# Delta-rule mixer: two chains over four groups in units of two tiles per direction, or four chains of 128 channels in units of one tile per direction

## The chip, the cores and the metric

The program runs on one core of a Trainium2 chip. The time is device microseconds from start to end of one execution. A core has TensorE (PE, with its weight loads listed as PEld), VectorE (DVE), ScalarE (ACT), GpSimd (POOL) and SyncE (SP, which issues the DMAs here). Each engine runs its own instructions in order, and the engines wait for one another through semaphores.

## The reference

Two transformer-like blocks are computed. The change lies in one mixer of the first block, a delta rule with decay (RWKV-7) over 8 heads of 64 channels, 256 context and 1024 latent tokens, run forwards (d = 0) and backwards (d = 1). The outputs of both directions are added and normed per head:

```python
def _rwkv7_scan(r, w, k, v, a, b, s0, reverse, emit):
    def step(s, inp):
        r_t, w_t, k_t, v_t, a_t, b_t = inp
        sa = jnp.einsum('bhvk,bhk->bhv', s, a_t)
        s = s * w_t[:, :, None, :] + sa[..., None] * b_t[:, :, None, :] + v_t[..., None] * k_t[:, :, None, :]
        y = jnp.einsum('bhvk,bhk->bhv', s, r_t) if emit else None
        return s, y
...
    y = ys[0] + ys[1]
    mu = jnp.mean(y, axis=-1, keepdims=True)
    var = jnp.mean(jnp.square(y - mu), axis=-1, keepdims=True)
    yn = ((y - mu) * lax.rsqrt(var + RW_GN_EPS)).reshape(bsz, l, RW_WIDTH) * lnx_g + lnx_b
    yn = yn + (bonus[0] + bonus[1]).reshape(bsz, l, RW_WIDTH)
    g = jax.nn.sigmoid(gd) @ g2
    return (yn * g).astype(r.dtype), (states[0], states[1])
```

## The kernel before

The program is a row of stages with a barrier between them (modulation, first projection, `rwkv_mix`, `hgrn_mix`, routing, experts, second block). Only `rwkv_mix` (tiles named rwmix_...) is touched. It is written out in full, without loops on the engines.

**Work.** Tokens are cut in chunks of 64. Within a chunk the recurrence is a triangular system. Its inverse is built in five levels by doubling: at each level `w` multiplies T by the masked X (tile W, plus the unit matrix), and `t` multiplies TT by W and W by TT to give the next T and its transpose TT. Then come w and u (tile wu), the matrices m and n by which a chunk changes the state, the state steps c0, c1, ..., and the outputs. Channels are cut in four groups of 128 (two heads each).

**Units.** A unit is a pair of tiles of each direction (4 chunks for each direction, 2 heads) of one group. Two chains, u = 0 and 1, each with its own half of PSUM, work off two groups one after the other, 5 units for each group, 20 units in all. Operations on DVE, ACT and POOL are mostly 128 partitions by 512 columns.

**Order.** A unit is a list of slots (`turn`, `prodb`, `prodk`, `zed`, `t0`, `w1`, `t1`, ..., `t5`, `wup`, `mn`, `intra`, `c0`, `query`, `c1`, `c2`, `c3`, `inter`). All engines walk the same interleaving (`interleaved`): one slot of chain 0, then one of chain 1, which is OFFSET = 11 slots behind. Below, one such step over all chains is called a round. A PE slot writes PSUM, and DVE or ACT copies the result to SBUF before the chain's next slot can run.

**Products.** Most matmuls are 64 by 64 with 64 columns. `crossed` (L1162) spreads them over the four quadrants of the array; `intra` (L1252, L1253), `zed` (L1211) and `wup` (L1172) use the two quadrants on the diagonal. The copies of T are on ACT (L1298), those of TT on DVE (L1370). The sums of outputs go through ACT (yi, L1313), POOL (L1469, second half of a group) and DVE (yacc, L1409).

**Norm.** When a group is done, the chain's last unit ends with the norm over all its 1024 tokens in slots `mean` to `gate`, in operations of 1024 columns (L1416 to L1432 on DVE, L1319 to L1328 on ACT, L1286 on PE, L1474 and L1476 on POOL); then SP stores the group.

**Loads.** SP loads a unit two ahead, tensor by tensor, 12 DMAs for each (L1129 to L1132), among them the decays of whole chunks (tot) in the layout in which DVE uses them.

## Time and profile before

| | us |
|---|---|
| median of three runs | 3963.1 (3958.7 to 3964.5) |
| span of the profiled execution | 3941.6 |
| so around the span | 21.5 |
| first DMA issue of `rwkv_mix` | 771.7 |
| first DMA issue of the next stage | 1358.7 |
| `rwkv_mix`, from one to the other | 587.0 |

The rows are from one profiled execution, and each time in them is counted from the start of its span. In a row of the timeline the first number is the start, the second the time until the last instruction of the row ends, `x` the number of instructions, and the bracket the idle time of that engine ahead of it with what ended it ("issue" is a wait for nothing that the profile shows). One float32 matmul of the code is two PE instructions in the trace, each with its own weight load; a transpose is one.

### The profile page before, as it was taken

How to read it: one execution, taken by the hardware profiler on the slowest of the kernel's cores; microseconds unless marked ns; L12 is line 12 of the kernel's file. 1: busy time of each engine (PE TensorE's matmuls, PEld its weight loads, DVE VectorE, ACT ScalarE, POOL GpSimd, SP SyncE). 2: the span in 40 equal slices, each digit the busy share in tenths (PEclk: the TensorE clock that was granted, in tenths of full speed). 3: DMA queues.
4: the chain of work that ended last, by engine and by line, in shares of the span. 5: the costliest groups of instructions: out<-in, count | busy, mean ns of one | idle time of the engine just before them, and what ended most of it. 6: DMA issues, size and time to landing. Idle time of an engine off the chain costs nothing. (4 is left out here: it accounts for less than half of the span.)

```text
span 3941.6 us, 97846 instructions
## 1 busy us (share of the span) xinstructions
PE 3377.2 (86%) x38463; PEld 2331.6 (59%) x38463; DVE 2360.6 (60%) x4245; ACT 1768.8 (45%) x2361; POOL 731.1 (19%) x706
## 2 busy tenths in 40 slices
PE   4999799677778587979998998999689999878789
PEld 0899788577677475733332333333267777666567
DVE  1688688655555466627776766776377574056631
ACT  0577577422222124307776766776222321156620
POOL 4000000043444200331221221222112333200000
PEclk7999899899899788989999999999899999988899
DMA  8354445421221255949889999953734323265452
GB/s 315 84 171 139 160 130 166 159 86 46 61 72 44 82 167 200 209 155 315 277 263 356 351 354 357 326 160 76 244 87 128 86 75 96 95 153 132 117 181 75
DMA packets 520291, 665.36 MB, mean 169 GB/s; under 512 B 77168, under 2 KB 423984, under 8 KB 516768
## 3 DMA queue, kind: packets, MB, share of 16 engines
q1 hardware_dynamic: 494576, 572.44, 45.2%
q0 software_dynamic: 25216, 86.62, 8.9%
q8 instruction: 312, 5.11, 0.5%
q14 instruction: 139, 1.14, 0.1%
q10 hardware_dynamic: 48, 0.05, 0.0%
HBM read 493.08 MB, written 165.94 MB: 167 GB/s over the span
## 5 line engine op out<-in xcount | busy, mean ns | idle before, releaser
L2600 PE MATMUL routed_p_gu<-routed_fixed,routed_x 128*32 128x512 f32 x3840 | 572.5, 600 | 0.0
L2600 PE MATMUL routed_p_gu<-moe_exp_w,routed_x 128*32 x1280 | 571.5, 600 | 0.7 <-DVE routed_fixed L2722 0.7
L2654 ACT COPY routed_fixed<-moe_exp_w 128x1024 f32 x320 | 332.6, 1047 | 222.1 <-DMA moe_exp_w<-in_exp_w_up_dram 86.3
L2722 DVE COPY routed_fixed<-moe_exp_w 128x1024 f32 x640 | 398.0, 681 | 51.3 <-DMA moe_exp_w<-in_exp_w_up_dram 42.9
L544 PE MATMUL front_ps<-front_a_high,front_w_high 128*128 128x320 f32 (+1 forms) x1120 | 362.7, 324 | 16.3 <-DVE front_w_low L797 13.4
L544 PE MATMUL front_ps<-front_a_low,front_w_high 128*128 128x320 f32 (+1 forms) x1120 | 353.8, 316 | 0.0
L544 PE MATMUL front_ps<-front_a_high,front_w_low 128*128 128x320 f32 (+1 forms) x1120 | 353.7, 316 | 0.0
L2600 PEld LDWEIGHTS routed_p_gu<-moe_exp_w,routed_x 128*32 128x32 f32 x1280 | 135.4, 111 | 356.2 <-issue 356.2
L3606 PE MATMUL pre_ps<-pre_a_high,pre_w_high 128*128 128x512 f32 x720 | 287.1, 399 | 13.3 <-ACT pre_xb L3753 6.7
L2615 PE MATMUL routed_p_y<-routed_wd,routed_hT 128*32 x640 | 290.4, 597 | 3.4 <-ACT routed_fixed L2665 3.4
L2615 PE MATMUL routed_p_y<-routed_fixed,routed_hT 128*32 128x512 f32 x1920 | 291.4, 597 | 0.0
L2734 DVE COPY routed_fixed<-routed_wd 128x1024 f32 x320 | 201.7, 691 | 141.2 <-PE routed_p_gu L2600 126.8
L3606 PE MATMUL pre_ps<-pre_a_high,pre_w_low 128*128 128x512 f32 x720 | 281.3, 391 | 0.0
L3606 PE MATMUL pre_ps<-pre_a_low,pre_w_high 128*128 128x512 f32 x720 | 281.2, 391 | 0.0
L2557 POOL DMA_INDIRECT total<-rw_mask,routed_yidx x80 | 128.6, 1608 | 732.2 <-ACT rw_mask L2671 604.6
L544 PEld LDWEIGHTS front_ps<-front_a_high,front_w_high 128*128 128x128 f32 x1120 | 213.3, 190 | 35.2 <-DVE front_w_low L797 18.0
L1445 POOL TENSOR_TENSOR rwmix_TT<-rwmix_at,rw_mask 64x256 f32<-64x256 f32 (+1 forms) x60 | 43.5, 725 | 922.4 <-DVE rwmix_at L1346 916.5
L544 PEld LDWEIGHTS front_ps<-front_a_low,front_w_high 128*128 128x128 f32 x1120 | 213.2, 190 | 1.3
L544 PEld LDWEIGHTS front_ps<-front_a_high,front_w_low 128*128 128x128 f32 x1120 | 213.0, 190 | 0.0
L2665 ACT COPY routed_fixed<-routed_wd 128x1024 f32 x160 | 167.1, 1047 | 47.4 <-PE routed_p_gu L2600 46.7
L2615 PEld LDWEIGHTS routed_p_y<-routed_wd,routed_hT 128*32 128x32 f32 x640 | 70.8, 111 | 196.9 <-issue 196.9
L3606 PEld LDWEIGHTS pre_ps<-pre_a_high,pre_w_high 128*128 128x128 f32 x720 | 135.9, 189 | 46.7 <-issue 16.5
(550 smaller groups left out, 7386.6 us busy)
## 6 DMA issues: line engine op xcount, KB each, us to landing
moe_exp_w<-in_exp_w_gate_dram SPq DMA_DIRECT2D x64, 1024.0 KB, 13.3
moe_exp_w<-in_exp_w_up_dram SPq DMA_DIRECT2D x64, 1024.0 KB, 16.4
routed_wd<-in_exp_w_down_dram SPq DMA_DIRECT2D x64, 1024.0 KB, 15.1
front_wt<-in_w_in_dram SPq DMA_DIRECT2D x70, 512.0 KB, 4.4
mod_w<-in_w_mod_dram SPq DMA_DIRECT2D x24, 1024.0 KB, 18.2
pre_wt<-in_w_in_dram SPq DMA_DIRECT2D x44, 512.0 KB, 4.0
out_a<-mix SPq DMA_DIRECT2D x24, 512.0 KB, 4.0
total<-out_none SPq DMA_DIRECT2D x24, 512.0 KB
```

The source lines that it names most:

```text
L544: op = nc.tensor.matmul(ps[:, s % 2, c, 0:size], w_part[:, s % 2, k, :], a_part[:, k, first + c * size:first + (c + 1) * size], start=(k = ...
L1445: nc.gpsimd.tensor_tensor(combos(TT[u][:])[to, es], combos(at[u][:])[at_rows, es], mask(MASK_LEVEL, at_rows, es), ALU.mult)
L2557: nc.gpsimd.indirect_dma_start(total, bass.IndirectOffsetOnAxis(ap=yidx[b % 2][:, :], axis=0), y[:, b % 2, :], None, compute_op=ALU.add).t ...
L2600: op = nc.tensor.matmul(p_gu[spot(s), :], x[:, b % 2, k, spot(s)], w, start=(k == 0), stop=(k == KD - 1))
L2615: op = nc.tensor.matmul(p_y[spot(s), h, :], hT[:, m, spot(s)], w, start=(m == 0), stop=(m == MT - 1))
L2654: nc.scalar.copy(fixed[:, place_of(b, c), 0, :], wgu[:, bass.ds(e % WS, 1), c * D:(c + 1) * D].rearrange("p o n -> p (o n)"))\
L2665: nc.scalar.copy(fixed[:, at, 0, :], wd[:, bass.ds(e % WD, 1), m, :].rearrange("p o n -> p (o n)"))\
L2722: op = nc.vector.tensor_copy(fixed[:, place_of(b, c), s - 1, :], wgu[:, bass.ds(es[s] % WS, 1), c * D:(c + 1) * D].rearrange("p o n -> p ( ...
L2734: op = nc.vector.tensor_copy(fixed[:, at, s - 1, :], wd[:, bass.ds(e % WD, 1), m, :].rearrange("p o n -> p (o n)"))
L3606: op = nc.tensor.matmul(ps[:, u, a:a + n], w_part[:, u, k, :], a_part[:, k, a:a + n], start=(k == 0 and j == 0), stop=(k == KD - 1 and j = ...
```

## The change

- **Chains.** Four chains, one for each group of 128 channels, each with two banks of PSUM, 5 slots apart (`OFFSET = 5`).
- **Units.** A unit is one tile of each direction (2 chunks for each direction): 10 units for each chain, then an eleventh that holds only a norm. Operations are 128 by 256 where they were 128 by 512, and there are twice as many.
- **State.** Two state steps for each unit (`c0`, `c1`), with both directions side by side on the two halves of the partitions.
- **Outputs.** The three products of an output (cb with u, ck with v, q with the state) add up in PSUM in slot `c1`; the copy through yi and its POOL addition are gone. They now all run on the two diagonal quadrants, as does the query product, and in `mn` the m products lie on the diagonal ones and the n products, twice as many, on the other two.
- **T and TT.** Both are written to one tile (`both`) by one ACT copy of 512 columns; the DVE copies of TT are gone.
- **Norm.** The norm of a unit's tiles is spread over the slots of the next unit, in operations of 256 columns (units 7 to 10, which then have 26 slots, the last one 8).
- **Loads.** a, b, r, k of one direction are one DMA. r is loaded once more in the layout of the state (`turned`). The decays are loaded once at the start by 16 DMAs and put in place by 40 POOL copies ahead of POOL's first mask, and the loads of lnx, for which ACT waits, come behind them.

```diff
-    OFFSET = 11
+    OFFSET = 5
...
         def slots(n):
-            out = ["turn", "prodb", "prodk", "zed", "t0"]
+            norm = ["mean", "square", "var", "root", "norm", "back", "res", "gate"] if finishing(n) else []
+            if n == TILES:
+                return norm
+            out = ["turn", "prod", "zed", "t0"] + norm[0:1]
             for l in range(1, LEVELS + 1):
-                out += [f"w{l}", f"t{l}"]
-            out += ["wup", "mn"] + (["intra"] if latent(n) else []) + ["c0"] + (["query"] if latent(n) else []) + ["c1", "c2"]
...
+                out += [f"w{l}"] + norm[2 * l - 1:2 * l] + [f"t{l}"] + norm[2 * l:2 * l + 1]
+            return out + ["wup", "mn", "c0", "c1"]
...
+            for u in range(GROUPS):
+                load(0, u)
+            load_totals()
             sp.dma_start(lnx[:, 0, :], column(par["lnx_g"])).then_inc(once, 16)
             sp.dma_start(lnx[:, 1, :], column(par["lnx_b"])).then_inc(once, 16)
...
+                            if step == 0:
+                                op = nc.tensor.matmul(b[half(c), 0, step_column(0, s, h)], wu[u][half(c), k, 0:HEAD],
+                                                      cb[u][half(c), k, :], start=True, stop=True)
+                            else:
+                                nc.tensor.matmul(y, cb[u][half(c), k, :], wu[u][half(c), k, HEAD:P], start=True, stop=False)
+                                nc.tensor.matmul(y, ck[u][half(c), k, :], vT[u][half(c), d, half(h)], start=False, stop=False)
+                                op = nc.tensor.matmul(y, q[u][half(c), s, h, :], S[u][half(c), z, s, h, :], start=False, stop=True)
...
+                elif p[0] == "t":
+                    to(both[u][:].rearrange("p w (f i) t -> p w f (i t)", f=2),
+                       both_banks(b, 2 * P, 2).rearrange("p f (w y) -> p w f y", w=2), p)
...
+                if p == "prod":
+                    if n == 0 and u == 0:
+                        pool.wait_ge(totals, 256)
+                        place_totals().then_inc(totals_placed, 1)
                     DV.wait(pool, by_vector[u], n, "at")
```

PE, in the first unit of chain 0 (the number at the end of a tile's name is the chain). Before, chain 0's state steps stand between the levels of chain 1:

```order
L1162 MATMUL rwmix_ps1<-rwmix_T1,rwmix_X1 64x64 [waits rwmix_by_scalar1,rwmix_by_pool1]
L1162 MATMUL rwmix_ps1<-rwmix_T1,rwmix_X1 64x64 x15
L1269 MATMUL rwmix_ps0<-rwmix_S0,rwmix_m0 64x64 [waits rwmix_by_vector0]
L1269 MATMUL rwmix_ps0<-rwmix_S0,rwmix_m0 64x64 x3
L1162 MATMUL rwmix_ps1<-rwmix_W1,rwmix_TT1 64x64 [waits rwmix_by_vector1]
L1162 MATMUL rwmix_ps1<-rwmix_W1,rwmix_TT1 64x64 x15
L1162 MATMUL rwmix_ps1<-rwmix_TT1,rwmix_W1 64x64 [waits rwmix_by_scalar1]
L1162 MATMUL rwmix_ps1<-rwmix_TT1,rwmix_W1 64x64 x15
L1269 MATMUL rwmix_ps0<-rwmix_S0,rwmix_m0 64x64 [waits rwmix_by_vector0]
L1269 MATMUL rwmix_ps0<-rwmix_S0,rwmix_m0 64x64 x3
```

and after it, from the same place of the first unit:

```order
L1294 MATMUL rwmix_ps0<-rwmix_S0,rwmix_m0 64x64 [waits rwmix_by_vector0]
L1294 MATMUL rwmix_ps0<-rwmix_S0,rwmix_m0 64x64 x3
L1221 MATMUL rwmix_ps1<-rwmix_both1,rwmix_X1 64x64 [waits rwmix_by_scalar1,rwmix_by_pool1]
L1221 MATMUL rwmix_ps1<-rwmix_both1,rwmix_X1 64x64 x7
L1221 MATMUL rwmix_ps2<-rwmix_W2,rwmix_both2 64x64 [waits rwmix_by_vector2]
L1221 MATMUL rwmix_ps2<-rwmix_W2,rwmix_both2 64x64 x7
L1221 MATMUL rwmix_ps2<-rwmix_both2,rwmix_W2 64x64 x8
L1250 MATMUL rwmix_ps3<-rwmix_vT3,rwmix_bkT3 64x64 [waits rwmix_by_vector3]
L1250 MATMUL rwmix_ps3<-rwmix_vT3,rwmix_bkT3 64x64 x7
L1233 MATMUL rwmix_ps0<-ident,rwmix_src0 128x128 [waits rwmix_by_vector0,rwmix_loaded01]
L1233 MATMUL rwmix_ps0<-ident,rwmix_src0 128x128 x7
```

A slot has half the matmuls that it had, and between a slot of a chain and that chain's next one there are slots of three other chains, not of one.

POOL at the start of the stage, before:

```order
L1445 TENSOR_TENSOR rwmix_TT<-rwmix_at,rw_mask 128x256
L1445 TENSOR_TENSOR rwmix_TT<-rwmix_at,rw_mask 64x256 x2
L1456 TENSOR_TENSOR rwmix_TT<-rwmix_TT,eye 128x512
L1441 TENSOR_TENSOR rwmix_X<-rwmix_at,rw_mask 128x512 x3
L1441 TENSOR_TENSOR rwmix_X<-rwmix_at,rw_mask 128x512 [waits rwmix_products0] x2
```

and after:

```order
L1455 COPY rwmix_tot<-rwmix_tot_raw 64x8 [waits rwmix_totals]
L1455 COPY rwmix_tot<-rwmix_tot_raw 64x8 x39
L1461 ISA [waits rwmix_by_vector0]
L1461 TENSOR_TENSOR rwmix_both<-rwmix_at,rw_mask 128x128
L1461 TENSOR_TENSOR rwmix_both<-rwmix_at,rw_mask 64x128 x2
L1474 TENSOR_TENSOR rwmix_both<-rwmix_both,eye 128x256
```

Forty copies, with a wait for the 16 loads of the decays, stand ahead of the first mask of chain 0.

## Rows read from the trace of the kernel before

**Rows 1.** Windows of `rwkv_mix`; columns: length, busy time (instructions) of engines, clock, DMA share.

```profile
796.30:1035.40 239.10, 193.33 (x7812) 176.55 (x7815) 132.21 (x292) 56.42 (x99) 91.86 (x88) 0.99 0.21 59
1035.40:1087.40 52.00, 36.89 (x1117) 32.99 (x1109) 32.32 (x59) 15.21 (x24) 22.40 (x17) 0.80 0.24 73
1087.40:1316.80 229.40, 184.21 (x7480) 168.05 (x7480) 127.70 (x283) 52.85 (x93) 90.26 (x86) 0.99 0.17 48
1316.80:1337.00 20.20, 15.52 (x416) 13.86 (x416) 11.32 (x22) 4.48 (x7) 3.13 (x3) 0.75 0.01 2
```

**Rows 2.** DMA view of the first three windows: instruction queue, packets, MB, share.

```profile
q8 instruction: 61, 1.00, 1.7%
...
q8 instruction: 9, 0.15, 1.2%
...
q8 instruction: 60, 0.98, 1.8%
```

**Rows 3.** Timeline of PE, 922.8 to 927 us, every row.

```profile
922.84 0.39 PE L1162 MATMUL rwmix_ps<-rwmix_T,rwmix_X 64*64 64x64 f32 x11 [0.76 <-issue]
923.01 0.27 PE L1260 MATMUL rwmix_ps<-rwmix_cb,rwmix_wu 64*64 64x64 f32 x3
923.07 0.22 PE L1162 MATMUL rwmix_ps<-rwmix_T,rwmix_X 64*64 64x64 f32 x1
923.07 0.68 PE L1260 MATMUL rwmix_ps<-rwmix_cb,rwmix_wu 64*64 64x64 f32 x29
924.07 0.69 PE L1162 MATMUL rwmix_ps<-rwmix_W,rwmix_TT 64*64 64x64 f32 x32 [0.32 <-DVE rwmix_W L1362]
924.58 0.65 PE L1162 MATMUL rwmix_ps<-rwmix_TT,rwmix_W 64*64 64x64 f32 x32
925.05 0.40 PE L1269 MATMUL rwmix_ps<-rwmix_S,rwmix_m 64*64 64x64 f32 x8
925.56 0.45 PE L1162 MATMUL rwmix_ps<-rwmix_T,rwmix_X 64*64 64x64 f32 x12
926.97 0.51 PE L1162 MATMUL rwmix_ps<-rwmix_T,rwmix_X 64*64 64x64 f32 x18 [0.97 <-issue]
```

**Rows 4.** Timeline of PE, 977 to 985 us: the rows that end an "issue" wait.

```profile
977.41 0.52 PE L1260 MATMUL rwmix_ps<-rwmix_cb,rwmix_wu 64*64 64x64 f32 x20 [1.13 <-issue]
...
981.03 0.39 PE L1269 MATMUL rwmix_ps<-rwmix_S,rwmix_m 64*64 64x64 f32 x6 [0.56 <-issue]
...
984.77 0.46 PE L1280 MATMUL rwmix_ps<-rwmix_S,rwmix_q 64*64 64x64 f32 x16 [1.10 <-issue]
```

**Rows 5.** Groups by shape, 772 to 1350 us: busy, mean ns | idle before, releaser.

```profile
L1211 PE MATMUL rwmix_ps<-rwmix_vT,rwmix_bkT 64*64 64x64 f32 x640 | 22.9, 220 | 7.3 <-DVE rwmix_ck L1346 6.4 <-issue 0.6
L1370 DVE COPY rwmix_TT<-rwmix_ps 128x256 f32<-128x256 f32 x160 | 60.4, 419 | 92.1 <-PE rwmix_ps L1162 91.9
L1445 POOL TENSOR_TENSOR rwmix_TT<-rwmix_at,rw_mask 128x256 f32<-128x256 f32 x20 | 14.6, 728 | 916.7 <-DVE rwmix_at L1346 916.5 <-issue 0.2
```

**Rows 6.** Timeline of the start of the stage, all engines.

```profile
775.41 0.43 SPq L1132 DMA_DIRECT2D rwmix_tot<-rw_tot  x1
...
786.45 2.45 POOL L1445 TENSOR_TENSOR rwmix_TT<-rwmix_at,rw_mask 128x256 f32<-128x256 f32 x3 [724.09 <-DVE rwmix_at L1346]
...
790.36 0.69 PE L1162 MATMUL rwmix_ps<-eye,rwmix_TT 64*64 64x64 f32 x32 [1.17 <-POOL rwmix_TT L1456]
...
791.85 0.35 PE L1162 MATMUL rwmix_ps<-rwmix_T,rwmix_X 64*64 64x64 f32 x9 [0.80 <-ACT rwmix_T L1298]
```

**Rows 7.** DMA issues of the whole run: count, KB each, median us to landing.

```profile
rwmix_tot<-rw_tot SPq DMA_DIRECT2D x40, 2.0 KB, 2.4
```

**Rows 8.** Groups of POOL: an operation on few elements of 64 partitions.

```profile
L150 POOL TENSOR_SCALAR_AFFINE_SELECT rw_mask<-rw_mask 64x32 f32<-64x32 f32 (+1 forms) x104 | 28.2, 272 | 13.6 <-issue 0.3
```

**Rows 9.** Timeline of the end of the stage: outputs of the last unit, last gate.

```profile
1336.84 0.75 DVE L1409 TENSOR_TENSOR rwmix_yacc<-rwmix_ps,rwmix_yi 128x256 f32<-128x256 f32 x2 [0.83 <-PE rwmix_ps L1280]
...
1351.89 2.34 POOL L1476 TENSOR_TENSOR rwmix_res<-rwmix_res,rwmix_bg 128x1024 f32<-128x1024 f32 x1
```

625 lines of the change are left out of this document (300 added, 325 removed).

## The prediction

> **What bounds the kernel now.** Only one stage changes, 587.0 us of the span of 3941.6, and a barrier stands on either side of it. So the question is what this stage costs. I read the windows of the stage first. In the long stretches PE is busy 193.33 of 239.10 us and 184.21 of 229.40 (81% and 80%), DVE 55%, POOL 38%, ACT 24% [rows 1]. PE leads, and a fifth of its time is idle. Four chains with half-size units look made to fill this fifth. So the next view is the timeline of PE, to see what the idle time is.
>
> Between 922.84 and 926.97 the rows count 11 + 3 + 1 + 29 + 32 + 32 + 8 + 12 = 128 matmuls [rows 3]. Both ends of this stretch are "issue" waits, of 0.76 and 0.97 us, and the second falls in the middle of a group of 32 whose operands are there. 128 matmuls with their weight loads are 256 instructions. The queue that brings instructions moved 61 packets, 1.00 MB in the first window, 16 KB each [rows 2], for 7812 + 7815 matmuls and weight loads [rows 1], so 256 of them for each packet. I read this as follows: PE uses up a block of 256 instructions and then waits for the next block. It uses 32 matmuls in 0.51 us (924.07 to 924.58) where all quadrants work [rows 3], so 128 in 2.04, far faster than blocks come. The block took 4.13 us, and three such waits elsewhere end 3.62 and 3.74 us apart [rows 4]. **The mean of the three, 3.83 us for a block, is my floor**, with 3.62 and 4.13 as its ends.
>
> How near the floor is the kernel already? 239.1 / 61 = 3.92 us for a block in the first window, 229.4 / 60 = 3.82 in the third, but 52.0 / 9 = 5.8 in the second, where the norm of the first two groups lies, and at the end 416 matmuls take 20.2 us, some 6.2 us for a block [rows 1, 2]. So the long stretches hang on the instruction stream, and the waits of PE for DVE (0.32 us in rows 3) lie within blocks that would have ended no earlier without them.
>
> The Trainium skill, "Runtime: NRT & Kernel Launch", section "Instruction fetch mechanics", speaks of refills in blocks of 16 KiB, 256 instructions, which rows 2 show too. It also says that the fetch is mostly hidden, because engines dispatch slower than it fills; rows 3 speak against that here. By its rule the forecast would be the first rival below.
>
> **The change, part by part.** Matmuls: a unit has 8 transposes, 16 products of `prod`, 8 each of `zed`, `t0` and `wup`, 112 of the levels, 24 of `mn`, 8 state products and, on latent tiles, 32 of query and output. In instructions of the trace that is 8 + 2 x 184 = 376 and 440; with 8 context units and 32 latent ones, 32 fewer for the last state step and 32 transposes of the norm it is 17088, exactly what the stage has now by the same count. The stream that must be fetched stays as long as it was: 135 blocks. Waits on two semaphores are written as an instruction of their own. I count 9 for each of 40 units, 360, where about 200 stand now: 0.6 block, **+2 us**.
>
> *Long stretches.* 61 blocks go from 3.92 to 3.83 us: **-5.5**. The third window is at the floor already: 0.
>
> *Norm in the middle.* It goes into the next units' slots, and its window falls from 52.0 to 9 x 3.83 = 34.5 us: **-17.5**. Its DVE work does not fall (from operations of 1024 columns to four times as many of 256) but DVE has 45% to spare.
>
> *Rounds with the norm in them.* The order is fixed, so a round lasts as long as its slowest chain. A copy of 256 columns takes 0.42 us [rows 5]. A level slot of half size is 0.26 of PE, 0.17 of emptying (0.69 less 0.51, rows 3), 0.42 and about 0.2 for two semaphores (0.80 idle for a 512-column copy, rows 6): 1.0 us, or 1.4 with two products and the wider copy. `prod` with its four masks is 2.7, `c1` 2.6, `turn` and `mn` 2.0, `c0` 1.7, `wup` 1.6. With chains 5 slots apart the slowest slots are 2.0, 2.7, 2.0, 1.7, 2.6 in five successive rounds, 2.2 in the mean, 40 us for 18 rounds. The floor for four units is 4 x 440 / 128 x 3.83 = 53 us, so there the rounds are hidden. The three units with the norm have 26 rounds, and by the same list these sum to 51 to 52. Two limits as close as 52 and 53 don't hide each other whole: **+8** for three units (0 to 25). Before, the same rule cost little, since 24 slots shared 55 us.
>
> *Quadrants.* Products on two quadrants take 22.9 / 640 = 36 ns [rows 5] where those on four take 16. Queries, state products of outputs and `mn` move some 25 instructions of a unit that way, 0.5 us for each unit, 20 us of PE. PE's work for a block rises from 193.33 / 61 = 3.17 to 3.3 us, still under 3.83. So it costs 0 as long as the floor holds, and 20 if it doesn't.
>
> *DVE and ACT.* DVE gives up the copies of TT (60 us, rows 5, and more of another shape) and gets many smaller operations in place of wide ones; ACT gets the copies. By my count DVE stays at 55 to 60% and ACT at 35%, both hidden under PE's stream.
>
> *Start.* SP issues 16 loads, 16 of decays and lnx behind them. At 0.43 to 0.48 us each [rows 6] the decays are issued by 787 and land by 789.3 with 2.4 us more [rows 7]. Then POOL makes 40 copies of 64 by 8. The nearest row is 0.272 us for 64 by 32 [rows 8]; the lower bound is 0.1 for a copy with an eighth of the work, and I take 0.15, 6 us (4 to 11). Then three masks, half of the 2.45 us before [rows 6] or a bit more, and one of 0.73 [rows 5]: `t0` runs at 797.4 and not at 790.36 [rows 6], **+7.0** (5 to 13). Ahead of it PE has done 56 matmuls, not 112: **+1.7**. Until all four chains run, 15 rounds pass with one to three: **+3**.
>
> *End.* The last window's 416 matmuls are 3.3 blocks, 12.4 us, and take 20.2: 8 us lost, since chains run out. After it the last chain has five rounds alone (t5, wup, mn, c0, c1: 8.9 us for 1.1 blocks), and the chain ahead of it costs 2.6 more: 8 again, 0. Then the norm: from 1336.84 to 1354.23 are 17.4 us [rows 9] in operations of 1024 columns. With 256 columns it lies between 17.4 / 4 = 4.4 and 17.4 / 2 = 8.7; I take 6.0, since each operation has a fixed part: **-11.4** (-8.7 to -13).
>
> *Loads.* r is loaded twice and rows are 512 bytes, not 1024: more packets, DMA share perhaps 0.3 where it is 0.21 [rows 1]. It is hidden: SP's queue is two units ahead, and behind its waits stand only loads that are needed 50 us later. It counts only if it lifts the floor: the first window (share 0.21) has 3.92, the third (0.17) 3.82.
>
> Sum: 2 - 5.5 - 17.5 + 8 + 7.0 + 1.7 + 3 - 11.4 = -12.7 us. The span becomes 3928.9, and with the 21.5 around it 3950.4: **3950 us**, 0.3% less.
>
> **The rivals.** *The floor is none* (0.13): the "issue" waits come from something else, and four chains fill PE. Then 135 blocks cost 3.3 us each, 70 us less than at 3.83: 3950 - 70 = 3880. For it: blocks with 3.62 in rows 4. Against it: the wait after exactly 128 matmuls with operands ready, and the third window that sits at the floor with twice the unit size. This is also what the page on the runtime would give.
>
> *The rounds bind* (0.17): the order is static, and four chains multiply the chances to be late. If every slot takes 25% more than in my list (DVE and POOL in order behind four chains, `prod` with four masks ahead of another chain's `wup`), 18 rounds take 50 us, which is just hidden, but 26 take 64 against 53: 33 for three units in place of 8, and the ramps 4 more. 3950 + 29 = 3979, slower. It decides from a mean of about 2.35 us for a round in the norm units.
>
> *The floor rises* (0.12): packets of other loads delay the instruction packets, and a block takes 3.92 as in the first window. 135 x 0.09 = 12: 3962, the same time.
>
> *The start is dearer* (0.08): POOL's copies at 0.27 us and norm units at +15: 3950 + 5 + 7 + 4 = 3966, within or just over the bound of slower.
>
> **How the numbers follow.** Forecast 0.50 (3935 to 3962 by its own bounds: floor at 3.75 to 3.9, norm units 0 to 15), of which 0.38 faster and 0.12 the same. With the rivals: faster 0.38 + 0.13 = 0.51; same 0.12 + 0.12 + 0.01 = 0.25; slower 0.17 + 0.07 = 0.24. The bound is 0.2% (8 us), about what a measurement of this kernel can tell from no change. Leaving out the first rival and the far end of the second gives the range 3915 to 3980: the low end is the floor at 3.62 with the rest as summed (135 x 0.21 = 28).
>
> **What would show it.** Right: the instruction queue's packets about 3.8 us apart throughout the stage, also between the old window of the norm; "issue" as the main wait of PE, and waits for DVE W nearly gone; `t0` of chain 0 some 25 us after the stage's first DMA; 10 to 11 us between the last output product and the next stage's first DMA. Wrong: packets 3.3 us apart or less (first rival); PE waiting for DVE and ACT in every round and packets 4.5 us apart in the last third (second); a stage as quick in its norm units as in the others would take away my +8.

## The result, and the profile after

The changed kernel takes 3980.0 us (median of five, 3977.2 to 3992.6) beside 3964.5 (3958.7 to 3968.1) for the kernel before on the same chip: a ratio of 1.0051, 95% interval 1.0034 to 1.0067. Later, on another chip, it was 3967.3 beside 3954.3, a ratio of 1.0035 (1.0023 to 1.0048). So it is slower by 0.35 to 0.5%: 13 and 15.5 us by the medians, 14 and 20 by the ratios, which go by the means. The forecast was 13 us less.

First the windows of the stage; length, busy time and instructions of PE, its weight loads, DVE, ACT and POOL, then clock, DMA share and GB/s, to be held against [rows 1]:

```profile
806.20:1033.00 226.80, 180.16 (x7026) 165.25 (x7028) 108.42 (x322) 76.62 (x177) 100.72 (x162) 1.00 0.21 56
1033.00:1204.00 171.00, 134.98 (x5198) 124.70 (x5200) 83.89 (x251) 54.08 (x125) 67.16 (x108) 1.00 0.27 74
1204.00:1340.00 136.00, 110.68 (x4040) 98.79 (x4032) 77.66 (x226) 48.87 (x117) 66.22 (x102) 1.00 0.21 55
```

The hole of the norm in the middle of the stage is gone (PE was busy 36.89 of 52.00 us there, now 79 to 81% in every window), yet no window is filled clearly better than the long ones of before (81 and 80%). The instruction queue of the same three windows, to be held against [rows 2]:

```profile
q8 instruction: 56, 0.92, 1.7%
...
q8 instruction: 41, 0.67, 1.7%
...
q8 instruction: 32, 0.52, 1.6%
```

That is 226.8 / 56 = 4.05, 171.0 / 41 = 4.17 and 136.0 / 32 = 4.25 us for a block of 256 instructions, where the forecast had 3.83. What PE waits for, summed from 806 to 1337 us (us in total, times, longest):

```profile
PE rwmix_ps L1221 <- issue: 54.1, 53, 2.1
PE rwmix_ps L1242 <- issue: 7.7, 6, 1.9
PE rwmix_ps L1250 <- DVE rwmix_ck L1374: 7.0, 12, 1.1
PE rwmix_ps L1294 <- issue: 5.3, 6, 1.6
...
PE rwmix_ps L1221 <- DVE rwmix_W L1388: 0.7, 1, 0.7
```

and in the kernel before, from 796 to 1337:

```profile
PE rwmix_ps L1162 <- DVE rwmix_W L1362: 31.0, 51, 2.0
PE rwmix_ps L1162 <- issue: 20.0, 25, 2.7
```

The wait for DVE W, 31.0 us before, is down to 0.7, as the four chains were to achieve. All waits of PE for DVE, ACT and POOL together fell from 65 to 23 us, and "issue" waits grew from 40 to 82: PE hangs on its instruction stream more than before, not less. With the instruction records of the trace counted off in blocks of 256, 85 of 113 us of PE's idle time between 806 and 1360 lie ahead of the first instructions of a block, where it was 43 of 111 before (796 to 1337).

The start, timelines of SP, ACT, PE and POOL (start, length; in brackets the idle time before and what ended it), beside [rows 6]:

```profile
781.73 10.40 SPq L1173 DMA_DIRECT2D rwmix_tot_raw<-rw_tot  x16
792.18 0.60 SPq L1192 DMA_DIRECT2D rwmix_lnx<-in_rw_lnx_g_dram  x1
...
795.07 0.37 ACT L1328 COPY rwmix_az<-rwmix_ps 128x256 f32<-128x256 f32 x1 [36.32 <-DMA rwmix_lnx<-in_rw_lnx_b_dram]
...
795.76 1.99 PE L1242 MATMUL rwmix_ps<-rwmix_src 64*64 64x128 f32 x32 [15.61 <-ACT rwmix_bT L1329]
...
793.67 5.57 POOL L1455 COPY rwmix_tot<-rwmix_tot_raw 64x8 f32<-64x8 f32 x40 [731.11 <-DMA rwmix_tot_raw<-rw_tot]
...
802.05 0.71 PE L1221 MATMUL rwmix_ps<-eye,rwmix_both 64*64 64x64 f32 x16 [1.64 <-POOL rwmix_both L1474]
```

And the end, timelines of DVE, POOL and SP: the output of the last unit, its last gate, the first load of the next stage, beside [rows 9]:

```profile
1371.05 0.42 DVE L1416 TENSOR_TENSOR rwmix_y<-rwmix_ps,rwmix_yacc 128x256 f32<-128x256 f32 x1 [2.77 <-PE rwmix_ps L1305]
...
1376.71 0.73 POOL L1486 TENSOR_TENSOR rwmix_res<-rwmix_res,rwmix_bg 128x256 f32<-128x256 f32 x1
...
1383.62 0.37 SPq L1571 DMA_DIRECT2D hgmix_src<-hg_kh  x1
```

From such rows the stage falls into three parts: from its first DMA to the first t0 product, from there to the end of the last output product, and from there to the first DMA of the next stage. I use this table for all kernels; blocks are the instruction packets between 830 and 1190 us. The parts are not independent, since a late start leaves less ramp to the middle. So one column goes by PE's work: the time from the stage's 1500th matmul in the trace to its 15500th (of 17088 in every kernel), which leaves out both ramps. One profile each, except where two are given.

| kernel | stage, us | to t0 | t0 to last product | matmul 1500 to 15500 | to next stage | blocks in 360 us | ratio to the kernel before |
|---|---|---|---|---|---|---|---|
| before | 587.0, 593.4 | 18.6, 18.9 | 546.4, 552.6 | 447.9, 454.3 | 22.0, 22.0 | 87, 86 | 1, 1.0001 |
| changed | 610.4, 598.0 | 28.8, 29.0 | 569.0, 556.1 | 459.8, 449.7 | 12.6, 12.9 | 87, 90 | 1.0051, 1.0035 |
| forecast | 574.3 | 25.6 | 538.1 | | 10.6 | 94 | 0.997 |
| changed, no reloads (a_once) | 575.9 | 28.3 | 535.1 | 429.5 | 12.5 | 94 | 0.9985 |
| no turned reloads (a_noturn) | 595.1 | 28.7 | 553.7 | 446.6 | 12.7 | 89 | 1.0023 |
| before, no reloads (b_once) | 588.6 | 19.6 | 547.0 | 443.1 | 22.0 | 88 | 0.9984 |
| waits of the start moved (a_start2) | 600.1 | 13.2 | 574.3 | 459.2 | 12.6 | 88 | 1.0027 |
| r turned by ACT (a_local) | 602.0 | 29.1 | 560.3 | 453.3 | 12.7 | 88 | 1.0043 |
| half-width products (a_narrow) | 599.9 | 28.6 | 558.8 | 451.2 | 12.5 | 90 | 1.0033 |
| before, loads split (b_split) | 595.0 | 23.0 | 550.0 | 451.8 | 22.0 | 86 | 1.0008 |
| before, loads in bursts (b_burst) | 595.7 | 18.9 | 554.9 | 451.2 | 22.0 | 86 | 1.0018 |
| loads of 64 KB (a_paced) | 596.1 | 39.4 | 544.0 | 439.2 | 12.7 | 92 | 1.0038 |
| loads one by one (a_spread) | 587.1 | 39.3 | 534.6 | 431.9 | 13.2 | 93 | 1.0029 |
| and start moved (a_spread2) | 581.5 | 14.5 | 554.4 | 433.0 | 12.6 | 94 | 1.0003 |
| and start mended (a_spread3) | 569.3 | 13.2 | 543.1 | 434.7 | 13.0 | 93 | 0.9974 |
| and r turned by ACT (a_spread4, again as a_spread4b) | 566.3, 564.3 | 12.9, 13.0 | 540.8, 538.7 | 431.1, 427.5 | 12.6, 12.6 | 94, 94 | 0.9957, 0.9957 |
| and chains three slots apart (a_spread5) | 563.7 | 13.1 | 536.8 | 433.3 | 13.8 | 93 | 0.9966 |

The two profiles of the kernel before differ by 6 us in the stage and those of the changed one by 12, so a difference of a few us in one row means little; the ratios, from 6 to 12 runs each in the later ones, carry the verdicts. Each ratio is to the kernel before on the same chip in the same round; the variants ran on several chips. Gains over the changed kernel are counted from its first ratio, 1.0051; from the second, 1.0035, each is 0.0016 or 6 us less.

### The profile page after: what moved, and what is told of

Read it like the earlier page. It is cut to its first block and busy times, and to the rows that moved or that the text cites. A ratio compares the mean times of both kernels' runs of the same rounds, so it can differ in the third digit from the quotient of the medians.

```text
span 3985.0 us, 98940 instructions
## 1 busy us (share of the span) xinstructions
PE 3398.6 (85%) x38463; PEld 2351.5 (59%) x38463; DVE 2338.7 (59%) x4434; ACT 1824.1 (46%) x2577; POOL 754.6 (19%) x934
## 5 line engine op out<-in xcount | busy, mean ns | idle before, releaser
L3616 PE MATMUL pre_ps<-pre_a_high,pre_w_high 128*128 128x512 f32 x720 | 287.1, 399 | 13.2 <-ACT pre_xb L3763 6.6
L1324 ACT COPY rwmix_both<-rwmix_ps 128x512 f32<-128x512 f32 (+1 forms) x240 | 121.7, 515 | 282.7 <-PE rwmix_ps L1221 278.0
L1443 POOL TENSOR_TENSOR rwmix_X<-rwmix_at,rw_mask 128x256 f32<-128x256 f32 x200 | 141.9, 731 | 201.2 <-PE rwmix_ps L1221 201.0
```

The costliest lines, as they stand in the source:

```text
L1324: nc.scalar.copy(out, in_).then_inc(by_scalar[u], 1)
L1443: nc.gpsimd.tensor_tensor(combos(X[u][:, l % 3]), combos(at[u][:]), mask(MASK_LEVEL + l), ALU.mult)\
L3616: op = nc.tensor.matmul(ps[:, u, a:a + n], w_part[:, u, k, :], a_part[:, k, a:a + n], start=(k == 0 and j == 0), stop=(k == KD - 1 and j = ...
```

## The experiments

**Are the loads hidden?** The list of blocks suggested that they are not. In the changed kernel I took each interval between two instruction packets from 830 to 1190 us and counted the packets of loads in it: 31 intervals with under 20 load packets last 3.78 us in the mean, 33 with 700 to 1200 last 4.26, and 12 with more last 4.65. One block of the last kind shows in PE's timeline:

```profile
944.90 0.27 PE L1221 MATMUL rwmix_ps<-rwmix_both,rwmix_W 64*64 64x64 f32 x2 [0.40 <-issue]
...
949.79 0.92 PE L1273 MATMUL rwmix_ps<-rwmix_az,rwmix_both 64*64 64x128 f32 x13 [0.85 <-issue]
```

Between these two rows the timeline has 126 matmuls, a block with its four semaphore instructions, in 4.89 us. A unit's loads run beside it. Here is the DMA view of 944 to 949 us in 40 slices of 0.125 us (busy tenths of the 16 DMA engines, GB/s):

```profile
DMA  0000000000013345799999999999756663122531
GB/s 0 0 0 0 0 0 0 0 0 0 0 61 102 111 135 143 229 328 352 340 348 316 336 344 324 307 283 426 221 164 193 168 154 86 41 43 55 109 80 14
```

For 1.4 us, eleven slices, all DMA engines are busy for 90% or more, mostly at 310 to 350 GB/s. But a unit's loads are also released by its `prod` products, so they may only coincide with slots that are dense in matmuls. The first experiment leaves them out:

```diff
-                    if n < TILES:
+                    if n < 2:
                         load(n, u)
-                        if latent(n):
-                            load_turned(n, u)
+                    if 2 <= n < 4:
+                        load_turned(n, u)
...
-                    pe.wait_ge(loaded[u][z], (n // 2 + 1) * (16 * LOADS))
+                    pe.wait_ge(loaded[u][z], 16 * LOADS)
...
-                        dve.wait_ge(r_loaded[u][z], ((n - CTX_TILES) // 2 + 1) * 64)
+                        dve.wait_ge(r_loaded[u][z], 64)
```

> The changed kernel with the reloads of its operands left out: each chain loads two tiles of each direction (and r, turned, for two latent ones) and all later units compute on these, so what is left out is 64 of 80 loads of 256 KB, 64 of 80 of 64 KB and 96 of 128 of 32 KB; PE, DVE, ACT and POOL do all that they did. In the changed kernel, up to the norm units, 34 blocks with under 20 packets of loads beside them take 3.87 us in the mean and 27 with over 1200 take 4.66. Theory A, bursts of loads delay the blocks: all blocks come to 3.9 us, and 31 bursts x 0.8 + 18 lesser ones x 0.35 = 31 us go, so 3980 becomes 3949 (3940 to 3957), ratio to the kernel before 0.996. Theory B, the bursts only fall into the slots that are dense in matmuls anyway: within 4 us of 3980, ratio 1.005.

Measured: 0.9985 (0.9971 to 0.9999), 0.66% or 26 us under the changed kernel's 1.0051, and 0.5% or 20 us under its 1.0035. Queues of loads (q1) and instructions (q8) from 830 to 1190 us, changed kernel first, then this one:

```profile
q1 hardware_dynamic: 53521, 22.21, 22.8%
q8 instruction: 87, 1.43, 1.7%
```

```profile
q1 hardware_dynamic: 10624, 3.94, 4.3%
q8 instruction: 94, 1.54, 1.8%
```

In the same 360 us 94 blocks pass in place of 87, 360 / 94 = 3.83 us each, which is the forecast's floor to the digit, and the stage lasts 575.9 us where 574.3 was forecast. Theory A holds in kind, though the ratio did not come down to its 0.996: the loads were not hidden.

The next one leaves out only the later loads of r in turned form (`load_turned` for n of 4 and more); b_once, its main edit shown below, leaves out all reloads in the kernel before.

> The changed kernel with only the 96 later loads of r in turned form (32 KB in packets of 256 bytes) left out; the outputs then use r of the first two latent tiles. Theory A with the number of packets as the measure: they are 512 of some 1800 packets of a unit's burst, so about a quarter to a third of the 31 us goes: 3970 (3968 to 3973). Theory A with SP's issue time as the measure (3.3 of 5.3 us of a unit's loads are these four): 3961. Theory B: 3980.

Measured: 1.0023 (1.0003 to 1.0043), 11 us under the changed kernel's 1.0051 (5 under 1.0035), in the range for the share of the packets and less than the 19 us for SP's issue time.

```diff
+                        if n >= 2:
+                            continue
                         for j, name in enumerate(("a", "r", "b", "k")):
                             sp.dma_start(src[u][:, z, j, d, :], rw[name][d, rows, tk]).then_inc(loaded[u][z], 16)
```

> The kernel before with the same part left out: each group loads two units, and all later units compute on these. In its trace the 84 blocks with under 20 packets of loads take 3.93 us, the 47 with more take 4.27. Theory A: 47 x 0.34 = 16 us go, ratio 0.996. Theory B: nothing, ratio 1.000. If the changed kernel without loads still stands 15 us over this one, loads are not what separates the two kernels.

Measured: 0.9984 (0.9971 to 0.9997), 6 us under the kernel before. That is less than the 16 us of Theory A. In the trace 0 to 6 us are won between t0 and the last product (547.0 against 546.4 and 552.6) and 5 to 11 in the column of matmuls. So the loads cost the kernel before some 6 us and the changed one 20 to 26, and without reloads the two kernels take the same time (0.9984 and 0.9985). The loads are what separates them.

**Is the stream the floor, or PE's work?** From the second tile on the level products move 32 columns:

```diff
-                        to = slice(first + i * HEAD, first + (i + 1) * HEAD)
+                        wide = HEAD if n == 0 else HEAD // 2
+                        to = slice(first + i * HEAD, first + i * HEAD + wide)
...
-                                                      rhs[half(at), rhs_at[k], :] if rhs is not None else consts["eye"][half(at), :],
+                                                      rhs[half(at), rhs_at[k], :] if rhs is not None and n == 0 else consts["eye"][half(at), 0:wide],
...
-                                                      S[u][half(c), z, s, h, :], start=True, stop=True)
+                                                      S[u][half(c), z, s, h, :] if n == 0 else consts["eye"][half(c), :], start=True, stop=True)
```

> The changed kernel with the same instructions and waits, but from the second tile on every product of the levels and of t0 moves 32 columns in place of 64 (of the identity), and the state step multiplies by the identity and not by the state: the results are not those of the delta rule, the number of instructions is the same. 8640 of the 17088 matmuls of the trace move half their columns. If the instruction stream is the floor, quiet blocks stay at 3.8 us and only blocks that were longer for their PE work shrink: 3960 to 3980, ratio 1.000 to 1.005. If the stage goes by PE's work (blocks dense in products longer than the stream), 8640 x 8 ns = 69 us of work go and at least 30 us of time: under 0.998.

Measured: 1.0033 (1.0018 to 1.0048), 7 us under 1.0051 and level with 1.0035. Half of the stage's matmuls are half as wide, and hardly anything is won; there are 90 blocks in 360 us, as in the second profile of the changed kernel. Windows 830 to 1190 of this kernel, and then of the changed one:

```profile
830.00:1190.00 360.00, 292.97 (x11315) 273.78 (x11316) 177.91 (x536) 118.78 (x274) 154.41 (x250) 0.98 0.26 68
```

```profile
830.00:1190.00 360.00, 282.80 (x11071) 260.97 (x11064) 173.00 (x520) 116.08 (x268) 150.34 (x242) 1.00 0.25 66
```

The test says less than its expectation took it to say. It counted on 8 ns less for each half-width matmul. In the trace an unbroken run of 64 level matmuls takes 0.94 us from its first start to its last in the changed kernel and 0.92 here: 15.0 and 14.5 ns from one to the next. So hardly any of PE's work was taken away, and PE counts as busy for 81% of the window here and for 79 and 81% in the two profiles of the changed kernel. That no time was won does not tell the stream from PE's work.

The instruction packets tell them apart. From 830 to 1190 us the two nearest start 3.2 to 3.4 us apart in each of the nineteen profiles, the shortest tenth of the intervals ends at 3.4 to 3.6 us, and the median is 3.7 to 4.0 us. PE itself is not so even: in a_once, one block in ten is followed by the next in 2.7 us or less. So the stream has a floor of its own. Where PE starts a block after an "issue" wait of over 0.3 us, the block's packet had started 2.5 us earlier, in every kernel, and the next packet starts 1.3 us later when no loads are beside it: 3.8 us together. "Runtime: NRT & Kernel Launch" of the Trainium skill, section "Instruction fetch mechanics", calls the cost of a 16 KiB boundary mostly hidden; these runs don't agree, with 85 of 113 us of PE's idle time at the starts of blocks.

**Does the burst do it, or the number of packets?** First the kernel before with the changed kernel's small packets, each load of 256 columns as two of 128:

```diff
-                            sp.dma_start(src[u][:, z, j, d, :], rw[name][d, rows, tk]).then_inc(loaded[u][z], 16)
...
+                        for e in range(2):
+                            te = slice(tk.start + e * P, tk.start + (e + 1) * P)
+                            to = slice(e * P, (e + 1) * P)
...
+                                sp.dma_start(src[u][:, z, j, d, to], rw[name][d, rows, te]).then_inc(loaded[u][z], 16)
```

> The kernel before, complete, with each load of 256 columns made as two of 128: packets of 512 bytes where there were 1024, twice as many packets and issues, the same bytes. If the number of packets in a burst delays the blocks (in the changed kernel with and without loads 26 us of 3980, in the kernel before 6 us), this costs about 6 us more than the kernel before has now, up to 15: ratio 1.0015 to 1.004. If bytes count and not packets: 1.000.

Measured: 1.0008 (0.9995 to 1.0020). Nearly twice as many packets cost 3 us, which can't be told from zero, and the number of packets alone falls as the cause of 20 to 26. The changed kernel differs in another way: it loads a, r, b and k of a direction in one DMA of 256 KB, so SP hands over a unit's 640 KB in 2 us. The next kernel makes ten loads of 64 KB of them:

```diff
-                    sp.dma_start(src[u][:, z, 0:4, d, :], rw["abrk"][d, :, rows, tk].rearrange("j p t -> p j t"))\
-                        .then_inc(loaded[u][z], 16)
+                    for j in range(4):
+                        sp.dma_start(src[u][:, z, j, d, :], rw["abrk"][d, j, rows, tk]).then_inc(loaded[u][z], 16)
```

> The changed kernel, complete, with each load of 256 KB made as four of 64 KB; packets stay 512 bytes and as many, but SP now issues ten loads for a unit at 0.43 us and more each instead of four, so a unit's 640 KB go out in over 4 us instead of 2. In the traces so far the changed kernel has up to 690 packets of loads in a microsecond and 84 to 90 microseconds with over 350, the kernel before 388 and 1, the one with split loads 385 and 4, and those two lose 3 to 6 us by their loads. Theory A2, a block's instruction packet waits behind a queue that is full, so the rate of the burst decides: blocks with a burst fall from 4.7 to 4.3 us, some 12 us: ratio 1.002 (1.001 to 1.003). Theory A1, the number of packets decides: 1.005, nothing changes. Theory C, longer bursts touch more blocks: 1.005 or more.

Measured: 1.0038 (1.0026 to 1.0050), outside the range of theory A2: 5 us under 1.0051 and none under 1.0035. The table says why: t0 now comes after 39.4 us, 10 later, since 40 loads stand ahead of the decays and lnx at the start. Matmuls 1500 to 15500 take 439.2 us where they took 459.8 and 449.7. Its queues from 830 to 1190 us:

```profile
q1 hardware_dynamic: 57787, 22.88, 24.1%
q8 instruction: 92, 1.51, 1.7%
```

As many packets and bytes as in the changed kernel, and 92 blocks.

The spread version goes further. SP walks through the rounds like the other engines and issues one load of the next unit behind `t0` and each level product, with the four of r turned in the last four of these slots:

```diff
+            at_slot = ["t0"] + [f"{w}{l}" for l in range(1, LEVELS + 1) for w in "wt"]
+            def body(n, p, u, b):
+                if p in at_slot and n + 1 < TILES:
+                    i = at_slot.index(p)
+                    PE.wait(sp, products[u], n, p)
...
+                    if i < 10:
+                        piece(n + 1, u, i)
+                    if latent(n + 1) and i >= 7:
+                        piece_turned(n + 1, u, i - 7)
```

> The changed kernel, complete, with the loads of the next unit issued one by one, each behind the level product of the same chain that it follows in the order (eleven slots, ten loads of 64 KB, the four of r turned in the last four), so that no more than 128 to 250 packets start together. Theory A2: nearly all of the 26 us that the loads cost goes, ratio 0.999 (0.998 to 1.001). Theory A1: 1.005. What speaks against a gain: SP now waits for PE some 440 times, and a load that comes late would stop a chain at turn.

Measured: 1.0029 (1.0012 to 1.0046), 9 us under 1.0051 and far from the 0.999 that was expected. The start again: 39.3 us to t0. Matmuls 1500 to 15500 take 431.9 us, near the 429.5 of the kernel with no reloads, with 93 blocks in 360 us. Theory A2 holds there; the expectation forgot that the first loads became forty.

The opposite test gives the kernel before the burst, with its packets of 1024 bytes and no more bytes (a, r, b and k lie in one tensor for it):

```diff
-                        for j, name in enumerate(("a", "r", "b", "k")):
-                            sp.dma_start(src[u][:, z, j, d, :], rw[name][d, rows, tk]).then_inc(loaded[u][z], 16)
+                        sp.dma_start(src[u][:, z, 0:4, d, :], rw["abrk"][d, :, rows, tk].rearrange("j p t -> p j t"))\
+                            .then_inc(loaded[u][z], 16)
```

> The kernel before, complete, with its four loads of 128 KB for a direction made as one of 512 KB, as the changed kernel does it (a, r, b and k lie in one tensor for that): bytes and packets (1024 bytes) are the same, but SP issues six DMAs for a unit's half in place of twelve, so the queue fills. In the changed kernel paced loads took t0 to the last product from 560 and 573 us to 548, and loads one by one to 539; the kernel before has 557 and 563 there, 558 with no reloads. If a full queue delays the instruction packets, this kernel loses what the changed one lost: blocks with over 350 packets of loads go from 4.3 to 4.6 or more, 35 x 0.3 = 10 us: 567 to 573 in the trace and a ratio of 1.002 to 1.004. If it is the small packets of 512 and 256 bytes that do it, 1.000.

Measured: 1.0018 (1.0007 to 1.0029), 7 us lost; the stage of the one profile, 595.7 us with 86 blocks in 360, is too near the two of the kernel before to show it. DMA view of this kernel from 930 to 960 us, in slices of 0.75 us:

```profile
DMA  0000100001000056974799000000000000001000
GB/s 0 0 0 0 22 0 0 0 0 22 0 0 0 0 79 183 363 239 63 202 384 282 2 0 0 0 22 0 0 0 0 22 0 0 0 0 22 0 0 0
```

Peaks of 363 and 384 GB/s stand where the kernel before issued its loads one after another. The small steps of 22 are single instruction packets, evenly spaced until the burst. So a burst alone, with large packets, makes the kernel before slower by the ratio; beside b_split's 1.0008 the difference is within the intervals.

The packets' own times show it better. For each "issue" wait of over 0.3 us (806 to 1345 us) I took the time from PE's start on the block to the start of the next instruction packet, and the load packets that start in the first 1.1 us of it. Mean us, number in brackets:

| kernel | under 20 load packets | 200 and more |
|---|---|---|
| before | 1.26 (39) | 1.79 (11) |
| b_burst | 1.21 (40) | 2.69 (9) |
| changed, two profiles | 1.30 (40), 1.24 (36) | 1.86 (27), 1.76 (28) |
| a_paced | 1.23 (13) | 1.56 (42) |
| a_spread | 1.44 (2) | 1.34 (34) |
| a_spread4 | 1.34 (10) | 1.26 (20) |

From the packet's start to PE's start on its block it is 2.46 to 2.58 us in the mean of each of them, and in the changed kernel 2.5 with and without loads beside it; the packets themselves take 1.06 to 1.14 us in the mean. So a burst holds up the instruction packet before it starts, by 0.5 us in the changed kernel and 1.5 in b_burst, and in a_spread and a_spread4, with loads one by one, no delay shows. The kernel before has the delay too, but in 11 of 50 such waits where the changed one has it in 27 of 79 and 28 of 76.

**The start.** Two waits are moved:

```diff
-            act.wait_ge(once, 32)
...
+                    if u == 0 and not second(n - 2):
+                        act.wait_ge(once, 32)
...
-                    if n == 0 and u == 0:
-                        pool.wait_ge(totals, 256)
-                        place_totals().then_inc(totals_placed, 1)
...
+                    if n == 0 and u == 0 and p == "w2":
+                        pool.wait_ge(totals, 256)
+                        pool.drain()
+                        place_totals().then_inc(totals_placed, 1)
+                        pool.drain()
```

A first form of this edit, without the two `pool.drain()`, gave no time (a_start).

> The changed kernel, complete, with two waits moved: ACT waits for lnx before its first norm output and no longer before its first copy, and POOL places the decays behind the sixth mask of the first chain and no longer before its first. In the changed kernel t0 of chain 0 runs at 802.05, 28.9 us after the stage's first load. If lnx and the decays set this, t0 comes at 788 to 790 and the stage is 12 us shorter: ratio to the changed kernel 0.997, so 1.002 to the kernel before. If the first operands themselves land late, or the ramp takes it back, under 3 us: 1.004 to 1.005.

Measured: 1.0027 (1.0013 to 1.0041), 10 us under 1.0051. t0 comes 15.6 us earlier (13.2 for 28.8), but the middle grows to 574.3, above both profiles of the changed kernel (569.0 and 556.1), so part of it is given back. Half is lost in the ramp, since the 1500th matmul comes only 8 us earlier; the column of matmuls, 459.2, is as before.

> The kernel of the run before with the two waits of the start moved as well (lnx, decays), which took 0.24% alone. If both add up: 0.9965 (0.995 to 0.998), 14 us under the kernel before. If the second tile's loads, now behind products of the ramp, come late, the gain of the start is lost: 0.999.

Measured: 1.0003 (0.9988 to 1.0018), outside the expected range on the slow side. What PE waits for from 780 to 860 us names what takes it back:

```profile
PE rwmix_ps L1244 <- POOL rwmix_both L1494: 17.2, 3, 16.1
```

POOL waits in the seventh round for decays that have not landed, and the first masks of chain 1 stand behind that wait. The next version moves this to the thirteenth round and makes the four first loads of the large DMAs again:

```diff
-                    if n == 0 and u == 0 and p == "w2":
-                        pool.wait_ge(totals, 256)
...
+                elif p == "w5" and n == 0 and u == 0:
+                    pool.wait_ge(totals, 256)
```

> The version with loads issued one by one and lnx awaited late (1.0003), with two repairs of the start: the four first loads are again made of the large DMAs, and the decays are placed in the thirteenth round, not the seventh, where PE waited 16.1 us once for POOL. Theory: those 16 us were the decays' landing, so 8 to 14 us go: ratio 0.997 (0.9965 to 0.9985). Rival: the ramp has other waits right behind this one, 0.9995 to 1.0005.

Measured: 0.9974 (0.9962 to 0.9987), 11 us less, as its theory had it: the middle falls from 554.4 to 543.1, and the column of matmuls stays (433.0 and 434.7).

**r turned on the chip.** ACT makes the turned r from the loaded one, ahead of its copies of the first two levels:

```diff
+                    if latent(n) and p in ("t1", "t2"):
+                        h = int(p[1]) - 1
+                        r = src[u][half(h), n % 2, 1]
+                        nc.scalar.copy(turned[u][half(0), n % 2, :, h], r[:, :, half(0)])
+                        for s in range(2):
+                            nc.scalar.copy(turned[u][half(1), n % 2, s, h], r[:, 1 - s, half(1)])
                     to(both[u][:].rearrange("p w (f i) t -> p w f (i t)", f=2),
                        both_banks(b, 2 * P, 2).rearrange("p f (w y) -> p w f y", w=2), p)
```

> The changed kernel, complete, with r turned on the chip: six ACT copies of 64 by 64 or 64 by 128 for each latent unit take the place of its four loads in packets of 256 bytes. Leaving those loads out brought the changed kernel from 1.0051 to 1.0023 of the kernel before. If ACT has room (it is 32% busy; 192 copies of some 0.25 us are 48 us more in 610), the same gain: 1.0025. If the copies delay the level copies behind them by 0.5 us in a round that binds: 1.005 or more.

Measured: 1.0043 (1.0025 to 1.0060), between the two theories and not to be told from no change. In the fastest version the same six copies stand behind the copies of the first three levels, so that no product waits for them:

> The same with r turned on the chip by six ACT copies behind the copies of the first three levels, so that the loads in packets of 256 bytes are gone. Blocks with 700 to 1200 packets beside them (4.08 us and 4.23 in the two spread versions, against 3.80 and 3.77 with 300 to 700) then lose their excess of 0.3 to 0.4 on some 45 blocks, if these loads are its cause: 10 us or more less than the run before, 0.995. If the copies delay ACT's level copies or the excess comes from elsewhere: the same as the run before, within 3 us.

Measured: 0.9957 (0.9943 to 0.9972), 7 us less than without, within the two intervals and short of the 10 us expected. It was run again:

> The same version with five slots, once more: 0.9957 (0.9943 to 0.9972) again, if that was its place.

Measured: 0.9957 (0.9938 to 0.9977), 3927.4 us beside 3943.3. This version is 17 us faster than the kernel before. Its DMA view from 944 to 949 us, beside the one of the changed kernel above, and its queues from 830 to 1190 us:

```profile
DMA  7562157200010000000064425641005000000000
GB/s 201 176 176 53 57 152 230 66 8 8 8 12 8 8 12 4 0 0 0 25 180 123 135 74 139 201 135 37 0 0 131 0 0 0 0 0 0 0 0 0
```

```profile
q1 hardware_dynamic: 43198, 19.75, 19.8%
q8 instruction: 94, 1.54, 1.9%
```

Five times the load bytes of the kernel without reloads (19.75 and 3.94 MB), and the same 94 blocks. It has 11% fewer bytes than the changed kernel (22.21 MB), so spreading is shown more cleanly by a_spread, which has them all.

**Chains three slots apart** (OFFSET = 3):

> The fastest version so far (0.9957: loads one by one, lnx late, decays in the thirteenth round, r turned on the chip) with the chains three slots apart in place of five: six rounds of the ramp go at the start and six at the end, so up to 12 us with one to three chains become 12 us shared by four. The stream is as long, so at best the ramp's loss (t0 to the last product 544.5 against 134 x 3.9 = 523, 21 us) falls by two fifths: 8 us, 0.994. If ends and starts of neighbouring chains (mn, c0, c1, turn, prod) now meet in one round and outlast the stream: 0.997 or more.

Measured: 0.9966 (0.9955 to 0.9977). The profile has 2 to 4 us less in the middle and 1 more in the tail; by the ratios it is 0.9966 beside 0.9957 on the same chip. Nothing is won, and the 8 us hoped for did not come.

**The two kernels once more.**

> The changed kernel as it is, once more, beside the variants and with a second profile. If 1.0051 (1.0034 to 1.0067) was its true place, this gives 1.004 to 1.006, and its stage lasts about 610 us in the trace. Should it give 1.003, half of what the variants seemed to win was chance.

Measured: 1.0035 (1.0023 to 1.0048), under the 1.004 expected but within the first interval. So the gains counted from 1.0051 are the upper ones: the reloads cost 20 to 26 us, and a_local, a_narrow and a_paced have won nothing that can be told from zero.

> The kernel before as it is, for a second profile: 1.000. Its stage lasted 587.0 us in the first. If it is within 3 us of that, stages of single profiles can be compared, and the stage alone explains the change: 610.4 - 587.0 = 23 us. If it is 595 or more, a good part of these 23 us is the spread of single executions.

Measured: 1.0001 (0.9992 to 1.0010), and a stage of 593.4 us, between the two cases. By the means of two profiles the stage is 14 us longer in the changed kernel (604.2 and 590.2), not 23, which agrees with the medians; the column of matmuls is 3.7 us longer (454.8 and 451.1).

## Why the prediction was wrong, step by step

**The step that failed is the one on loads**, "It is hidden", costed at 0. It did name the condition ("It counts only if it lifts the floor"), and the rival that the floor rises had the mechanism, packets of loads that delay the instruction packets. But that rival took its size from the first window's 3.92 us against 3.82 in the third. These come from dividing by whole packets; by PE's instructions, semaphore instructions included, the two windows are 61.4 and 58.8 blocks, 3.89 and 3.90 us each, so the rows held no price of loads at all. And the changed kernel issues other loads: one DMA of 256 KB for four tensors, and with it all DMA engines busy at up to 350 GB/s. The rival's 12 us were 20 to 26. I had looked at SP's queue for whether the loads come in time, and counted packets and shares (0.25 of the DMA engines from 830 to 1190 us, 0.3 forecast); neither shows a burst. The mean share says nothing on how long the queue is when the instruction packet arrives.

**The floor of 3.83 us** for a block was right as a mean, with its cause: 94 blocks in 360 us with no reloads. It came from three stretches only, and the hard limit lies lower, at 3.2 to 3.4 us between packets, in all kernels. The first rival, that the floor is none and a block takes 3.3 us in the mean, falls with the spacing of the packets; a_narrow could not decide it.

**Long stretches and the norm in the middle**: the sum was right, but paid back by the loads. By the 3.89 and 3.90 us above the third window was no nearer the floor than the first: -4 for each of them in place of -5.5 and 0. With no reloads the time from t0 to the last product is 535.1 us, and the terms -5.5, -17.5, +2, +8, +1.7 and +3 made it 538.1. That tells of their sum; none of them was tried by itself.

**Semaphores**: 360 were counted, and the trace has 364 between 806 and 1360 us.

**Norm units, +8**: with no reloads 120 us ahead of them (1045 to 1165) take 32 packets of instructions and 120 us within them (1180 to 1300) take 30:

```profile
q8 instruction: 32, 0.52, 1.9%
...
q8 instruction: 30, 0.49, 1.6%
```

3.75 and 4.0 us for a block; over the 32 blocks of the last window (1204 to 1340 us) 8 us. One packet more or less would make this 4 or 12, so it bears the +8 out only roughly. The rounds don't bind beyond that, so the second rival falls, and that its 3979 us is the time that was measured is chance: its signs were waits of PE for DVE and ACT in every round, which came to 19 us in all, and 4.5 us for a block in the last third, where it was 4.25 with the loads and 4.0 without.

**Quadrants, 0**: not tried by itself, and no run here shows it.

**Start, +7.0**: it was +10.2 (28.8 against 18.6). The copies of POOL are 5.57 / 40 = 0.14 us each, where 0.15 was taken, so that choice was right. Two things were missed. SP takes 10.40 / 16 = 0.65 us to issue a load of decays, not 0.43 to 0.48 as in [rows 6]. And ACT's first instruction waits for lnx, which now stands behind all of them (36.32 us idle, until 795.07); the prediction listed lnx in SP's queue and never asked who waits for it.

**End, -11.4**: it was -9.4. The norm of the last unit, 1371.05 to 1377.44, takes 6.4 us for the 6.0 taken; the way from the last gate to the next stage's first DMA grew from 4.5 to 6.2 us, behind the last stores.

**The range.** Its low end, 3915, does not follow from its own sum: 3950 less 28 is 3922. Nothing hung on it.

**The base.** The sum took 21.5 us to lie around the span. The spans and times of later runs of one execution differ by 1.7 us only (3985.0 and 3986.7): the profile of before was an execution 20 us faster than the median. This did no harm, since the forecast was in effect the median less 12.7, but single profiles were trusted too far.

Together: -12.7 + 20 to 26 (loads) + 3 (start) + 2 (end) = +12 to +18, beside +14 to +20 measured by the ratios. The loads are shown by leaving them out, and the burst from both sides (a_paced and a_spread take it away, b_burst brings it). The times of the packets show where the loss lies: the instruction packet starts later when a burst is under way. That it stands behind load packets in the same queues is the reading that fits; the trace has no record of the moment when it is asked for.

What stays open: the stages that the change doesn't touch take 3352 to 3361 us in the five profiles of kernels like the one before and 3353 to 3375 in the fourteen of kernels like the changed one. The medians of before and changed leave no room for it (+14 us of stage, +13 to +15.5 in all), those of a_spread4 would leave some 8 us. I did not find its cause.

## What to carry to other kernels

Where an engine runs dense small instructions, look at the spacing of its instruction packets first: if "issue" waits come at the starts of blocks, the stream is the bound, and bursts of data DMAs delay it, however well hidden they are from the operands' side. Then spread the loads: many single ones behind the work of the chain, rather than one large DMA that fills the queue, although the large one costs SP fewer issues. And when loads are reordered at a stage's start, ask for each one in the queue who waits for it, down to constants that are needed only much later.

## What the runs showed of the hardware

- A burst of loads slows the instruction stream of another engine. In the changed kernel the intervals between instruction packets grew from 3.78 us (under 20 load packets beside them) to 4.65 (over 1200). In a_spread4, which issues its loads one by one (19.75 MB for 22.21 in 360 us), they were 3.87 us in the mean with under 700 load packets (79 of 93) and 3.73 with more (14).
- The loss lies ahead of the packet: 1.2 to 1.3 us from PE's start on a block to the next packet without loads, 1.8 to 1.9 in a burst of the changed kernel, 2.7 in b_burst; from there to PE's next start after a wait 2.5 us in all.
- No two instruction packets of PE started less than 3.2 us apart between 830 and 1190 us, in nineteen profiles.
- The number of packets did little: 42908 for 23891 in 360 us of the kernel before, with the same bytes, gave a ratio of 1.0008 (0.9995 to 1.0020).
- SP's issue time depends on the form of the load: 0.43 us in [rows 6], 0.65 for the decays, 3.06 / 4 = 0.77 for r turned (946.39 us in the timeline).
- Level matmuls of 64 by 64 on four quadrants started 15.0 ns apart; with 32 columns for 64, 14.5 ns. PE's busy share stayed near 80%.
